# Front end of a decoder layer: which vectors are loaded first, from which queue, and TensorE given work on a zeroed tile

## The chip, the cores and the metric

One Trainium2 chip, one of its cores. The metric is the device time of one execution in microseconds. Five engines of the core run their own instruction streams and meet at semaphores: TensorE (PE), VectorE (DVE), ScalarE (ACT), GpSimd (POOL) and SyncE (SP). SP, ACT and POOL can issue DMA transfers.

## The reference, cut to what matters

One layer of a decoder with 256 tokens and 2048 channels, in float32:

```python
u = rms_norm(x, mix_norm_pre)            # over channels, then a gain per channel
proj = u @ w_in
c_q, c_kv, k_r, z, xbc, dt_raw, g_attn, g_ssm = split_cols(proj, IN_SPLITS)
attn = mla_branch(c_q, c_kv, k_r, cos, sin, q_norm, w_uq, kv_norm, w_ukv)
ssm = mamba2_branch(z, xbc, dt_raw, conv_w, conv_b, dt_bias, a_log, d_skip, ssm_norm)
mixed = sigmoid(g_attn) * (attn @ w_attn_o) + sigmoid(g_ssm) * (ssm @ w_ssm_o)
h = x + rms_norm(mixed @ w_out, mix_norm_post)
# then a SwiGLU block (ffn_norm_pre, ffn_norm_post) and a gated
# embedding block (ple_norm_pre, ple_norm_post), each added to h
```

The first part of the state-space branch puts a causal convolution of width 4 (`conv_w`, `conv_b`) on the columns x, B and C of the projection.

## The kernel before, in words

Activations are held with channels on the 128 partitions and the 256 tokens beside them. `u` has 16 such tiles, each twice: `u[:, kt, 0]` is the rounded high part (float32r), `u[:, kt, 1]` the remainder. Weights come in chunks of [128, 1024] floats through a ring of four slots (`raw`): ScalarE writes the high part `whi`, VectorE the remainder `wlo`, and TensorE does three matmuls for each tile (`mm3`: high by high, high by low, low by high). Chunks are worked off in an order written out by hand in `PHASES`: first "bc" (4 chunks, the B and C columns of one group), then "ssm" (8 rounds of 20 chunks; the first four of round 0 are half as wide and hold the rope and dt columns), then the others. Each engine's stream names the chunks in this order and puts its other work between them. SP loads chunk n when `lo_ready` says that VectorE has split chunk n − 4; TensorE begins a chunk when it has been split. "bc" chunks are loaded without a wait.

The front end works like this. SP loads x, tokens on partitions, as four transfers (`x_tok`, two blocks of 128 tokens, two halves of columns; semaphores `x_in00` to `x_in11`), then the first "bc" chunk, then eight transfers of parameter vectors into `rows`, then the other weights. ACT's queue loads the constants (`cst`: identity, triangle, ones) and four more vectors; POOL's queue loads three vectors of the heads (`dtb`, `alog`, `dsk`). For each block of tokens ScalarE and VectorE sum the squares of one half of the columns each (L944, L1356), the inverse root follows (L935, L937, `newton` at L1345 to L1347), and VectorE puts it on a diagonal, `dg` (L1366). TensorE multiplies x by this diagonal, which transposes and scales at once (`x_transposed`, L475): seven banks of PSUM for block 0, then block 1, the eighth bank at the end. Bank 7 is used in between for four transposes of `rows` (L488), which bring all parameter vectors onto the partitions. VectorE copies them to `pv_all` (L1369) and the 104 columns that are kept to `pv` (L1371). With them ScalarE makes `u` high (L956) and VectorE `u` low (L1376), two tiles a bank, with the splits of the four "bc" chunks (L926, L1325) between them. Then VectorE clears `xdt` (L1384), rearranges the convolution's parameters from `pv_all` into `gp_all` (L1387 to L1397), and only then splits the first "ssm" chunk. TensorE does the "bc" chunks and goes on to `rope_dt_chunk`; the dt columns are transposed in bank 7 (L516). At the start, TensorE's queue raises 13 semaphores (L430).

Of the kernel before, what the change touches and what calls it, by code (L numbers as in the profile page):

```python
# [49 lines left out]
P = 128  # L50
# [30 lines left out]
V_KEEP = 104  # L81
V_CB, V_SN, V_TAP = 104, 152, 184
V_ALL = 376
# [9 lines left out]
def build(nc, x, p_in, positions, mix_norm_pre, mix_norm_post, w_in, q_norm, w_uq, kv_norm, w_ukv,  # L93
# [60 lines left out]
    sq_tok = first("sq_tok", [P, D_MODEL])  # L154
    dg = first("dg", [P, 2, P])
    rows = first("rows", [P, 4, P])
    pv_all = first("pv_all", [P, V_ALL])
# [68 lines left out]
    def bank(b):  # L226
        return psum[:, b, :]
# [118 lines left out]
    def _(sp):  # L346
# [8 lines left out]

        vec = [(ffn_norm_pre, 16, 32), (ffn_norm_post, 16, 48), (ple_norm_pre, 16, 64), (ple_norm_post, 16, 80)]
        for v, n, at_row in vec:
            sp.dma_start(rows[at_row:at_row + n, 0, :], v.rearrange("(t p) -> t p", p=P)) \
                .then_inc(sem("rows_in"), 16)
        sp.dma_start(rows[0:48, 1, :], conv_b.rearrange("(t p) -> t p", p=P)).then_inc(sem("rows_in"), 16)  # L360
        sp.dma_start(rows[48:80, 1, :], ssm_norm.rearrange("(t p) -> t p", p=P)).then_inc(sem("rows_in"), 16)
        for i in range(2):
            sp.dma_start(rows[0:96, 2 + i, :],
                         conv_w[2 * i:2 * i + 2, :].rearrange("a (t p) -> (a t) p", p=P)) \
                .then_inc(sem("rows_in"), 16)
        for phase, (per, its) in PHASES.items():
# [31 lines left out]
    @block.gpsimd  # L398
    def _(pool):
        for v, dst in ((dt_bias, dtb), (a_log, alog), (d_skip, dsk)):  # L400
            pool.dma_start(dst[:, :], v.partition_broadcast(P)).then_inc(sem("heads_in"), 16)
# [26 lines left out]
    def _(pe):  # L428
# [43 lines left out]
        def x_transposed(b, blk):  # L472
# [5 lines left out]
            if blk:  # L478
                last.then_inc(sem("xt_mm"), 1)

        pe.wait_ge(sem("dg_ready"), 1)
        for b in range(7):
            x_transposed(b, 0)
        pe.wait_ge(sem("cst_in"), 16)
        pe.wait_ge(sem("rows_in"), 12 * 16)
        at_col = 0
        for i, n in enumerate((V_KEEP, 80, 96, 96)):
            last = T.transpose(bank(7)[:, at_col:at_col + n], rows[0:n, i, :], cst[0:n, 0:n])  # L488
            at_col += n
        last.then_inc(sem("pv_mm"), 1)  # L490
        pe.wait_ge(sem("dg_ready"), 2)
# [6 lines left out]
        for c_ in range(4):  # L498
            pe.wait_ge(sem("u_lo"), 4 * c_ + 4)
            chunk("bc", 0, c_, (0, 1), u, range(4 * c_, 4 * c_ + 4), c_ == 0, c_ == 3)  # L500

        def rope_dt_chunk(c_):
# [9 lines left out]
        def dt_by_tokens():  # L512

            pe.wait_ge(sem("kr_ev"), 1)
            for blk in range(2):
                last = T.transpose(bank(7)[:, 64 * blk:64 * blk + 64], kr[64:P, blk * P:blk * P + P], cst[64:P, 64:P])  # L516
            last.then_inc(sem("dt_mm"), 1)
# [395 lines left out]
    def _(act):  # L913
        S.preload_act_table_set("natural_log_exp_and_others")
        act.dma_start(cst[:, :], cst_in).then_inc(sem("cst_in"), 16)
        for v, n, at_row in ((mix_norm_pre, 16, 0), (mix_norm_post, 16, 16), (q_norm, 4, 96), (kv_norm, 4, 100)):
            act.dma_start(rows[at_row:at_row + n, 0, :], v.rearrange("(t p) -> t p", p=P)) \
                .then_inc(sem("rows_in"), 16)

# [32 lines left out]
        for b in range(8):  # L952
            act.wait_ge(sem("xt_mm"), b + 1)
            for k in range(2):
                kt = 2 * b + k
                S.activation(u[:, kt, 0, :], bank(b)[:, k * SEQ:k * SEQ + SEQ], ACT.Identity,  # L956
                                 scale=pv_all[:, V_MIXPRE + kt:V_MIXPRE + kt + 1]).then_inc(sem("u_hi"), 1)
            if b in (0, 2, 4, 6):
                split("bc", 0, b // 2)
# [360 lines left out]
    def _(dve):  # L1320
# [31 lines left out]


        for b in range(2):
            dve.wait_ge(sem(f"x_in{b}1"), 16)
# [8 lines left out]
            if b == 0:  # L1364
                dve.wait_ge(sem("cst_in"), 16)
            V.tensor_scalar(dg[:, b, :], ident, st0[:, b, 4:5], None, ALU.mult).then_inc(sem("dg_ready"), 1)  # L1366

        dve.wait_ge(sem("pv_mm"), 1)
        V.tensor_copy(pv_all[:, :], bank(7)[:, 0:V_ALL]).then_inc(sem("pv_ev"), 1)  # L1369
        dve.wait_ge(sem("pv_ev"), 1)  # L1370
        V.tensor_copy(pv[:, :], pv_all[:, 0:V_KEEP]).then_inc(sem("pv_kept"), 1)  # L1371
        for b in range(8):
            dve.wait_ge(sem("u_hi"), 2 * b + 2)
            for k in range(2):
                kt = 2 * b + k
                V.scalar_tensor_tensor(u[:, kt, 1, :], bank(b)[:, k * SEQ:k * SEQ + SEQ],  # L1376
                                           pv_all[:, V_MIXPRE + kt:V_MIXPRE + kt + 1],
                                           u[:, kt, 0, :].bitcast(F32), ALU.mult, ALU.subtract) \
                                               .then_inc(sem("u_lo"), 1)
# [3 lines left out]

        link(V.memset(xdt[:, :, :, 64:128], 0.0))  # L1384
        taps = pv_all[:, V_TAP:V_ALL].rearrange("p (a n) -> p a n", a=4)
        gp_taps = gp_all[:, :, 0:24].rearrange("p g (a t) -> p a g t", t=6)
# [649 lines left out]
```

## Time and profile before

| | |
|---|---|
| median of 3 runs | 2198.53 us (2197.8 to 2199.4) |
| profiled execution | 2199.38 us |
| its span, first to last instruction | 2197.6 us |
| TensorE busy | 2149.7 us, 98% of the span |
| VectorE, ScalarE busy | 1326.4 us (60%), 1075.8 us (49%) |
| mean granted TensorE clock | 0.993 |

In rows of the timeline an instruction stands as start, duration, engine, line of the kernel, operation, output<-input with shapes, and a count if several follow each other; in brackets how long the engine was idle before it and what released it. A float32 matmul leaves two records. TensorE overlaps instructions, so a record's duration is longer than the distance to the next.

### The profile page before, as it was taken

How to read it: one execution, taken by the hardware profiler on the slowest of the kernel's cores; microseconds unless marked ns; L12 is line 12 of the kernel's file. 1: busy time of each engine (PE TensorE's matmuls, PEld its weight loads, DVE VectorE, ACT ScalarE, POOL GpSimd, SP SyncE). 2: the span in 40 equal slices, each digit the busy share in tenths (PEclk: the TensorE clock that was granted, in tenths of full speed). 3: DMA queues.
4: the chain of work that ended last, by engine and by line, in shares of the span. 5: the costliest groups of instructions: out<-in, count | busy, mean ns of one | idle time of the engine just before them, and what ended most of it. 6: DMA issues, size and time to landing. Idle time of an engine off the chain costs nothing.

```text
span 2197.6 us, 41147 instructions
## 1 busy us (share of the span) xinstructions
PE 2149.7 (98%) x15558; PEld 2033.8 (93%) x15558; DVE 1326.4 (60%) x1902; ACT 1075.8 (49%) x1311; POOL 9.6 (0%) x21
## 2 busy tenths in 40 slices
PE   7999999999999999999999989999999999999997
PEld 7999999999999999999999978888888888888896
DVE  5767777767664444676455457566666664444655
ACT  5555556555554444344444455444444444344653
POOL 0000000000000000000000000000000000000000
PEclk9999999999999999999999999999999999999998
DMA  7665665555555555445556535666666655555452
GB/s 208 192 177 161 187 185 163 174 179 162 172 174 182 179 183 177 125 120 161 183 182 213 189 115 170 192 187 189 188 191 186 191 189 183 184 182 193 152 163 86
DMA packets 411419, 382.85 MB, mean 174 GB/s; under 512 B 25864, under 2 KB 407296, under 8 KB 410080
## 3 DMA queue, kind: packets, MB, share of 16 engines
q1 hardware_dynamic: 409360, 370.37, 55.3%
q0 software_dynamic: 1776, 11.44, 1.6%
q8 instruction: 41, 0.67, 0.1%
q10 hardware_dynamic: 224, 0.22, 0.0%
q14 instruction: 18, 0.15, 0.0%
HBM read 379.81 MB, written 2.16 MB: 174 GB/s over the span
## 4 chain that ended last, share of the span: by engine, by line
PE 95%; DVE 2%; ACT 1%; issue 1%; DMA 0%; SPq 0%; ACTq 0%; DVEq 0%
PE acc L454 22%; PE acc L434 18%; PE acc L436 18%; PE acc L435 18%; PE acc L456 11%; PE acc L727 1%; PE acc L799 1%; PE acc L552 1%; PE acc L558 1%; PE acc L563 1%; PE acc L661 0%; PE acc L662 0%; DVE wlo L1325 0%; ACT whi L926 0%; DVE bt L1850 0%
## 5 line engine op out<-in xcount | busy, mean ns | idle before, releaser
L1325 DVE TENSOR_TENSOR wlo<-raw,whi 128x1024 fp32r<-128x1024 f32 (+1 forms) x712 | 853.1, 1202 | 660.8 <-ACT whi L926 658.2
L926 ACT ACTIVATE whi<-raw 128x1024 fp32r<-128x1024 f32 (+1 forms) x712 | 735.6, 1040 | 668.0 <-PE acc L436 386.8
L434 PE MATMUL acc<-u,whi 128*128 128x256 f32 x2192 | 630.6, 288 | 2.9 <-DVE wlo L1325 1.7
L436 PE MATMUL acc<-u,wlo 128*128 128x256 f32 x2192 | 620.3, 283 | 0.0
L435 PE MATMUL acc<-u,whi 128*128 128x256 f32 x2192 | 620.2, 283 | 0.0
L454 PE MATMUL acc<-u,whi 128*128 128x512 f32 x1408 | 490.2, 395 | 0.0
L434 PEld LDWEIGHTS acc<-u,whi 128*128 128x128 f32 x2192 | 420.5, 192 | 5.5 <-DVE wlo L1325 1.6
L435 PEld LDWEIGHTS acc<-u,whi 128*128 128x128 f32 x2192 | 420.4, 192 | 1.2
L436 PEld LDWEIGHTS acc<-u,wlo 128*128 128x128 f32 x2192 | 420.3, 192 | 0.0
L456 PE MATMUL acc<-u,wlo 128*128 128x256 f32 x1408 | 390.5, 277 | 0.0
L454 PEld LDWEIGHTS acc<-u,whi 128*128 128x128 f32 x1408 | 264.6, 188 | 61.4
L434 PE MATMUL acc<-g,whi 128*128 128x256 f32 x1024 | 290.9, 284 | 2.5 <-DVE wlo L1325 2.5
L436 PE MATMUL acc<-g,wlo 128*128 128x256 f32 x1024 | 289.8, 283 | 0.0
L435 PE MATMUL acc<-g,whi 128*128 128x256 f32 x1024 | 289.8, 283 | 0.0
L456 PEld LDWEIGHTS acc<-u,wlo 128*128 128x128 f32 x1408 | 264.8, 188 | 0.2
L454 PE MATMUL acc<-g,whi 128*128 128x512 f32 x704 | 248.4, 398 | 1.5 <-issue 1.5
L434 PEld LDWEIGHTS acc<-g,whi 128*128 128x128 f32 x1024 | 196.5, 192 | 3.4 <-DVE wlo L1325 3.3
L456 PE MATMUL acc<-g,wlo 128*128 128x256 f32 x704 | 197.7, 281 | 0.0
L435 PEld LDWEIGHTS acc<-g,whi 128*128 128x128 f32 x1024 | 196.5, 192 | 0.0
L436 PEld LDWEIGHTS acc<-g,wlo 128*128 128x128 f32 x1024 | 196.5, 192 | 0.0
L454 PEld LDWEIGHTS acc<-g,whi 128*128 128x128 f32 x704 | 132.2, 188 | 34.3 <-issue 1.8
L456 PEld LDWEIGHTS acc<-g,wlo 128*128 128x128 f32 x704 | 133.0, 189 | 0.0
(277 smaller groups left out, 1610.7 us busy)
## 6 DMA issues: line engine op xcount, KB each, us to landing
raw<-w_in_in SPq DMA_DIRECT2D x208, 512.0 KB, 3.8
raw<-w_gate_in SPq DMA_DIRECT2D x88, 512.0 KB, 4.3
raw<-w_up_in SPq DMA_DIRECT2D x88, 512.0 KB, 4.5
raw<-w_ssm_o_in SPq DMA_DIRECT2D x64, 512.0 KB, 3.5
raw<-w_down_in SPq DMA_DIRECT2D x64, 512.0 KB, 3.5
raw<-w_in_in SPq DMA_DIRECT2D x64, 256.0 KB, 4.0
raw<-w_attn_o_in SPq DMA_DIRECT2D x32, 512.0 KB, 3.5
raw<-w_out_in SPq DMA_DIRECT2D x32, 512.0 KB, 4.5
```

Source lines behind the costliest of these rows:

```text
L434: T.matmul(o, wh, xh, start=start, stop=False, skip_group_check=True)
L435: T.matmul(o, wh, xl, start=False, stop=False, skip_group_check=True)
L436: return T.matmul(o, wl, xh, start=False, stop=stop, skip_group_check=True)
L454: T.matmul(bank(b), wh[:, j, i * P:i * P + P], src[:, kt, :, :].rearrange("p a s -> p (a s)"), start=start and j == 0, stop=False, skip_gr ...
L456: last = T.matmul(bank(b)[:, 0:SEQ], wl[:, j, i * P:i * P + P], src[:, kt, 0, :], start=False, stop=stop and j == len(kts) - 1, skip_group ...
L552: T.matmul(bank(b)[:, 0:256], xdt[:, 0, p, 0:128], ea[:, 0:256], start=True, stop=False, skip_group_check=True)
L558: T.matmul(bank(b)[:, 0:256], xdt[:, 0, p, 64:192], eb[:, 0:256], start=False, stop=True, skip_group_check=True).then_inc(sem("y_mm"), 1)
L563: last = T.matmul(bank(7)[:, 0:256], ones, sq[:, t, :], start=t == 0, stop=t == 3)
L727: last = T.matmul(o, c[:, 4 + j, a_, t], w_[:, j, :], start=j == 0 and blk == 0 and n_ == 0, stop=j == 3 and n_ == 2 and blk == 1, skip_gr ...
L799: last = T.matmul(bank(6)[:, 0:SEQ], ones, sq_n[:, j % 2, i, :], start=j == 0 and i == 0, stop=j == 7 and i == 1, skip_group_check=True)
L926: S.activation(whi[:, slot, 0:w], raw[:, slot, 0:w], ACT.Copy).then_inc(sem("hi_ready"), 1)
L1325: V.tensor_tensor(wlo[:, slot, 0:w], raw[:, slot, 0:w], whi[:, slot, 0:w].bitcast(F32), ALU.subtract) \
```

## The change

Of the parameter vectors, only `mix_norm_pre` is loaded at the start (ACT's queue, its own semaphore `pre_in`). The eleven other transfers into `rows` go to POOL's queue, ahead of the three head vectors, and POOL issues them when the last quarter of x is in. TensorE gets 32 matmuls on a tile `warm` that VectorE sets to zero, then transposes `mix_norm_pre` alone, then the x blocks. VectorE copies the 16 columns of `mix_norm_pre` between `dg` 0 and block 1. The four transposes of `rows` come after the "bc" chunks on TensorE, and the copies of `pv_all` and `pv` after the clearing of `xdt` on VectorE. `dt_by_tokens` waits for the copy too, since it writes bank 7. ScalarE and VectorE take the gain of `u` from `pv`.

```diff
@@ -153,6 +153,7 @@
     x_tok = first("x_tok", [P, 2, D_MODEL])
     sq_tok = first("sq_tok", [P, D_MODEL])
     dg = first("dg", [P, 2, P])
+    warm = first("warm", [P, P])
     rows = first("rows", [P, 4, P])
     pv_all = first("pv_all", [P, V_ALL])
     st0 = first("st0", [P, 2, 8])
@@ -353,16 +354,6 @@
             sp.dma_start(raw[:, 0, :].rearrange("p (t n) -> p t n", t=4)[:, :, o:o + STATE], src) \
                 .then_inc(raw_in[0], 16)
 
-        vec = [(ffn_norm_pre, 16, 32), (ffn_norm_post, 16, 48), (ple_norm_pre, 16, 64), (ple_norm_post, 16, 80)]
-        for v, n, at_row in vec:
-            sp.dma_start(rows[at_row:at_row + n, 0, :], v.rearrange("(t p) -> t p", p=P)) \
-                .then_inc(sem("rows_in"), 16)
-        sp.dma_start(rows[0:48, 1, :], conv_b.rearrange("(t p) -> t p", p=P)).then_inc(sem("rows_in"), 16)
-        sp.dma_start(rows[48:80, 1, :], ssm_norm.rearrange("(t p) -> t p", p=P)).then_inc(sem("rows_in"), 16)
-        for i in range(2):
-            sp.dma_start(rows[0:96, 2 + i, :],
-                         conv_w[2 * i:2 * i + 2, :].rearrange("a (t p) -> (a t) p", p=P)) \
-                .then_inc(sem("rows_in"), 16)
         for phase, (per, its) in PHASES.items():
             def load(it, c):
                 slot = c % RING
@@ -397,6 +388,18 @@
 
     @block.gpsimd
     def _(pool):
+        pool.wait_ge(sem("x_in11"), 16)
+        vec = [(mix_norm_post, 16, 16), (ffn_norm_pre, 16, 32), (ffn_norm_post, 16, 48), (ple_norm_pre, 16, 64),
+               (ple_norm_post, 16, 80), (q_norm, 4, 96), (kv_norm, 4, 100)]
+        for v, n, at_row in vec:
+            pool.dma_start(rows[at_row:at_row + n, 0, :], v.rearrange("(t p) -> t p", p=P)) \
+                .then_inc(sem("rows_in"), 16)
+        pool.dma_start(rows[0:48, 1, :], conv_b.rearrange("(t p) -> t p", p=P)).then_inc(sem("rows_in"), 16)
+        pool.dma_start(rows[48:80, 1, :], ssm_norm.rearrange("(t p) -> t p", p=P)).then_inc(sem("rows_in"), 16)
+        for i in range(2):
+            pool.dma_start(rows[0:96, 2 + i, :],
+                           conv_w[2 * i:2 * i + 2, :].rearrange("a (t p) -> (a t) p", p=P)) \
+                .then_inc(sem("rows_in"), 16)
         for v, dst in ((dt_bias, dtb), (a_log, alog), (d_skip, dsk)):
             pool.dma_start(dst[:, :], v.partition_broadcast(P)).then_inc(sem("heads_in"), 16)
 
@@ -478,16 +481,15 @@
             if blk:
                 last.then_inc(sem("xt_mm"), 1)
 
+        pe.wait_ge(sem("warm_set"), 1)
+        for _ in range(32):
+            T.matmul(bank(7)[:, 0:P], warm[:, :], warm[:, :], start=True, stop=True)
+        pe.wait_ge(sem("cst_in"), 16)
+        pe.wait_ge(sem("pre_in"), 16)
+        T.transpose(bank(7)[:, 0:16], rows[0:16, 0, :], cst[0:16, 0:16]).then_inc(sem("pv_mm"), 1)
         pe.wait_ge(sem("dg_ready"), 1)
         for b in range(7):
             x_transposed(b, 0)
-        pe.wait_ge(sem("cst_in"), 16)
-        pe.wait_ge(sem("rows_in"), 12 * 16)
-        at_col = 0
-        for i, n in enumerate((V_KEEP, 80, 96, 96)):
-            last = T.transpose(bank(7)[:, at_col:at_col + n], rows[0:n, i, :], cst[0:n, 0:n])
-            at_col += n
-        last.then_inc(sem("pv_mm"), 1)
         pe.wait_ge(sem("dg_ready"), 2)
         for b in range(7):
             x_transposed(b, 1)
@@ -498,6 +500,13 @@
         for c_ in range(4):
             pe.wait_ge(sem("u_lo"), 4 * c_ + 4)
             chunk("bc", 0, c_, (0, 1), u, range(4 * c_, 4 * c_ + 4), c_ == 0, c_ == 3)
+
+        pe.wait_ge(sem("rows_in"), 11 * 16)
+        at_col = 0
+        for i, n in enumerate((V_KEEP, 80, 96, 96)):
+            last = T.transpose(bank(7)[:, at_col:at_col + n], rows[0:n, i, :], cst[0:n, 0:n])
+            at_col += n
+        last.then_inc(sem("pv_mm"), 1)
 
         def rope_dt_chunk(c_):
 
@@ -512,6 +521,7 @@
         def dt_by_tokens():
 
             pe.wait_ge(sem("kr_ev"), 1)
+            pe.wait_ge(sem("pv_ev"), 2)
             for blk in range(2):
                 last = T.transpose(bank(7)[:, 64 * blk:64 * blk + 64], kr[64:P, blk * P:blk * P + P], cst[64:P, 64:P])
             last.then_inc(sem("dt_mm"), 1)
@@ -913,9 +923,7 @@
     def _(act):
         S.preload_act_table_set("natural_log_exp_and_others")
         act.dma_start(cst[:, :], cst_in).then_inc(sem("cst_in"), 16)
-        for v, n, at_row in ((mix_norm_pre, 16, 0), (mix_norm_post, 16, 16), (q_norm, 4, 96), (kv_norm, 4, 100)):
-            act.dma_start(rows[at_row:at_row + n, 0, :], v.rearrange("(t p) -> t p", p=P)) \
-                .then_inc(sem("rows_in"), 16)
+        act.dma_start(rows[0:16, 0, :], mix_norm_pre.rearrange("(t p) -> t p", p=P)).then_inc(sem("pre_in"), 16)
 
         def split(phase, it, c):
 
@@ -954,7 +962,7 @@
             for k in range(2):
                 kt = 2 * b + k
                 S.activation(u[:, kt, 0, :], bank(b)[:, k * SEQ:k * SEQ + SEQ], ACT.Identity,
-                                 scale=pv_all[:, V_MIXPRE + kt:V_MIXPRE + kt + 1]).then_inc(sem("u_hi"), 1)
+                                 scale=pv[:, V_MIXPRE + kt:V_MIXPRE + kt + 1]).then_inc(sem("u_hi"), 1)
             if b in (0, 2, 4, 6):
                 split("bc", 0, b // 2)
 
@@ -1351,6 +1359,7 @@
                 link(ins)
 
 
+        V.memset(warm[:, :], 0.0).then_inc(sem("warm_set"), 1)
         for b in range(2):
             dve.wait_ge(sem(f"x_in{b}1"), 16)
             link(V.tensor_tensor_reduce(out=sq_tok[:, 1024:2048], in0=x_tok[:, b, 1024:2048],
@@ -1364,17 +1373,17 @@
             if b == 0:
                 dve.wait_ge(sem("cst_in"), 16)
             V.tensor_scalar(dg[:, b, :], ident, st0[:, b, 4:5], None, ALU.mult).then_inc(sem("dg_ready"), 1)
-
-        dve.wait_ge(sem("pv_mm"), 1)
-        V.tensor_copy(pv_all[:, :], bank(7)[:, 0:V_ALL]).then_inc(sem("pv_ev"), 1)
+            if b == 0:
+                dve.wait_ge(sem("pv_mm"), 1)
+                V.tensor_copy(pv[:, 0:16], bank(7)[:, 0:16]).then_inc(sem("pv_ev"), 1)
+
         dve.wait_ge(sem("pv_ev"), 1)
-        V.tensor_copy(pv[:, :], pv_all[:, 0:V_KEEP]).then_inc(sem("pv_kept"), 1)
         for b in range(8):
             dve.wait_ge(sem("u_hi"), 2 * b + 2)
             for k in range(2):
                 kt = 2 * b + k
                 V.scalar_tensor_tensor(u[:, kt, 1, :], bank(b)[:, k * SEQ:k * SEQ + SEQ],
-                                           pv_all[:, V_MIXPRE + kt:V_MIXPRE + kt + 1],
+                                           pv[:, V_MIXPRE + kt:V_MIXPRE + kt + 1],
                                            u[:, kt, 0, :].bitcast(F32), ALU.mult, ALU.subtract) \
                                                .then_inc(sem("u_lo"), 1)
             if b in (0, 2, 4, 6):
@@ -1382,6 +1391,10 @@
 
 
         link(V.memset(xdt[:, :, :, 64:128], 0.0))
+        dve.wait_ge(sem("pv_mm"), 2)
+        V.tensor_copy(pv_all[:, :], bank(7)[:, 0:V_ALL]).then_inc(sem("pv_ev"), 1)
+        dve.wait_ge(sem("pv_ev"), 2)
+        link(V.tensor_copy(pv[:, 16:V_KEEP], pv_all[:, 16:V_KEEP]))
         taps = pv_all[:, V_TAP:V_ALL].rearrange("p (a n) -> p a n", a=4)
         gp_taps = gp_all[:, :, 0:24].rearrange("p g (a t) -> p a g t", t=6)
         V.tensor_copy(gp_taps[:, :, :, 0:4], taps[:, :, 0:32].rearrange("p a (g t) -> p a g t", t=4))
```

## Rows read from the trace of the kernel before

**Rows 1.** The page, part 1: busy time, share of the span and instructions.

```profile
PE 2149.7 (98%) x15558; PEld 2033.8 (93%) x15558; DVE 1326.4 (60%) x1902; ACT 1075.8 (49%) x1311; POOL 9.6 (0%) x21
```

**Rows 2.** TensorE's waits over the whole span, longest first.

```profile
PE acc L475 <- DVE dg L1366: 11.1, 1, 11.1
```

**Rows 3.** The chain of waits, 0 to 60 us: start, us, what.

```profile
1.33 6.80 DMA x_tok<-x_in
...
11.07 6.29 PE acc L475 x28
17.36 0.34 PE acc L488 x4
17.73 0.56 DVE pv_all L1369
18.31 0.84 ACT u L956 x2
...
22.19 0.39 PE acc L434
```

**Rows 4.** Instructions in order of time, 12 to 34 us: start, us, what.

```profile
12.55 1.23 DVE L1356 CUSTOM_DVE_ANT_0 sq_tok<-x_tok 128x1024 f32<-128x1024 f32 x1 [1.54 <-DMA x_tok<-x_in]
...
15.12 0.28 DVE L1366 TENSOR_SCALAR dg<-cst,st 128x128 f32<-128x128 f32 x1
...
17.20 0.49 PE L488 MATMUL acc<-cst,rows 104*128 104x104 f32 x4
...
18.31 0.21 DVE L1371 COPY pv<-pv_all 128x104 f32<-128x104 f32 x1
...
33.81 0.28 PE L434 MATMUL acc<-u,whi 128*128 128x256 f32 x1
```

**Rows 5.** VectorE, then ScalarE, in order of time, 30 to 38 us.

```profile
30.82 0.23 DVE L1387 COPY gp_all<-pv_all 128x128 f32<-128x128 f32 x1
...
31.87 0.69 DVE L1325 TENSOR_TENSOR wlo<-raw,whi 128x512 fp32r<-128x512 f32 x1
...
37.39 1.22 DVE L1325 TENSOR_TENSOR wlo<-raw,whi 128x1024 fp32r<-128x1024 f32 x1 [1.96 <-ACT whi L926]
...
36.30 1.06 ACT L926 ACTIVATE whi<-raw 128x1024 fp32r<-128x1024 f32 x1 [1.59 <-DMA raw<-w_in_in]
```

**Rows 6.** L475 alone in two stretches: length, PE busy, PEld busy, PEclk, DMA, GB/s.

```profile
11.07:17.36 6.29, 6.29 (x28) 6.04 (x28) 1.00 1.14 269
17.53:21.74 4.21, 4.21 (x36) 4.02 (x36) 1.00 0.43 107
```

**Rows 7.** Instructions in order of time, around 1305 and 2175 us.

```profile
1304.63 2.05 PE L799 MATMUL acc<-sq_n,cst 128*128 128x256 f32 x4 [8.64 <-ACT sq_n L1185]
...
1307.00 2.08 PE L799 MATMUL acc<-sq_n,cst 128*128 128x256 f32 x4 [0.32 <-ACT sq_n L1185]
...
2175.22 1.13 PE L837 MATMUL acc<-sq_n,cst 128*128 128x256 f32 x4 [1.97 <-ACT sq_n L1290]
```

**Rows 8.** Stretches: busy time by engine, then PEclk, DMA share and GB/s.

```profile
1299.00:1301.00 2.00, 0.00 (x0) 0.00 (x0) 0.89 (x3) 1.00 (x2) 0.00 (x0) 0.90 0.71 239
1310.00:1311.00 1.00, 1.00 (x5) 0.90 (x4) 1.00 (x3) 0.00 (x0) 0.00 (x0) 0.58 0.06 16
...
2175.00:2180.00 5.00, 1.13 (x4) 0.68 (x4) 1.33 (x4) 3.57 (x5) 0.00 (x0) 0.78 0.00 0
```

**Rows 9.** The source line L430 alone: durations in ns, first and last start.

```profile
L430 PEldq EVENT_SEMAPHORE  x13: 51/51/51, 1.0 to 2.8; - x13
```

**Rows 10.** Instructions in order of time, 117 to 119 us.

```profile
117.58 1.22 DVE L1325 TENSOR_TENSOR wlo<-raw,whi 128x1024 fp32r<-128x1024 f32 x1 [0.65 <-ACT whi L926]
117.61 0.55 POOL L408 DMA_DIRECT2D cumb<-cum_scratch  x1 [39.53 <-DVE e L1465]
```

**Rows 11.** DMA issues, 0 to 120 us: size of one, median us to landing.

```profile
cum_scratch<-cumt POOLq DMA_DIRECT2D x1, 64.0 KB, 3.2
...
dsk<-d_skip_in POOLq DMA_DIRECT2D x1, 32.0 KB, 8.1
```

## The prediction

> **What bounds the kernel now.** I read the page's busy shares first. TensorE is busy for 98% of the span [rows 1], so nearly all of the time is one dense stream of matmuls. A change to the front end can only shift the start of that stream or put holes in it. Next I read TensorE's waits: the longest, 11.1 us, stands before its first instruction [rows 2]. Then the chain of waits over the front [rows 3], to see which work fills the time before the main stream. It runs: x from DRAM to 8.19 us, the sum of squares and its root on VectorE and ScalarE, the first diagonal `dg`, 28 TensorE records on L475 from 11.07 for 6.29 us, the row transposes (L488), the copy of `pv_all` at 17.73, the first two `u` tiles on ScalarE at 18.31, one weight split on each of ScalarE and VectorE, two `u_lo` tiles, and the first main matmul at 22.19. From there matmuls start every 0.12 us to the end of the "bc" work (96 of them), and the rope/dt chunk follows at 33.81 without a gap [rows 4]. The last reading is what VectorE does between, since the change moves work into that place: it finishes `u_lo`, clears `xdt`, fills `gp_all` from 30.82 to 31.87 and has the first rope/dt split ready at about 32.56, 1.25 us before TensorE needs it [rows 5].
>
> **The change part by part.**
>
> *The work on the zeroed tile.* The first 14 diagonal matmuls (28 records) take 11.07 to 17.20, 0.438 us each; the last 18 (36 records) take 4.21 us, 0.234 each [rows 6]. The granted clock in the profile reads 1.00 in both stretches, but the pace of the first is about half that of the second, as between 1.2 and 2.4 GHz. The engine had been idle before the first, and had worked 6.13 us when the pace rose. Later in the trace the clock is seen at 0.50 while matmuls restart at 1304.63; from 1307.00 they run nearly without a stop, and in the stretch 1310 to 1311 the clock reads 0.58, so it rose at about 1310.84, 3.84 us after 1307.00 [rows 7, 8]. I take these two as bounds for the slow stretch of the new work and 5 us, about their middle, as its value.
>
> TensorE can't start at zero: its queue is busy with 13 semaphore instructions whose last starts at 2.8 [rows 9], so the new work begins at 2.85. (The memset of `warm` on an idle VectorE is over well before.) With 5 us slow, 11.4 matmuls are done at 7.85 and the other 20.6 take 4.82 us: end at 12.67. With 3.84 us the end is at 12.1, with 6.13 at 13.2. Then the one transpose of `mix_norm_pre` and its copy on VectorE: no row has either; from the start of the four L488 transposes to the copy of their result 0.53 us pass (17.20 to 17.73), and the smallest copy there takes 0.21 [rows 3, 4]. I take 0.35 and 0.20, 0.55 together, so the vector is ready at 13.2 (12.65 to 13.75).
>
> *VectorE's new wait.* That wait stands between `dg` 0 and the sum of squares of the second half of x. Before, this sum starts at 12.55, when x lands [rows 4]. Behind it are the mean, the root and `dg` 1, ready at 15.40, 2.85 us later. Now it starts at 13.2: 0.67 us later (0.1 to 1.2). If x lands sooner because fewer small transfers lie beside it, it changes nothing, since the copy is later. The transposes of the first half of x, 14 at 0.234, run from 12.7 to 16.0 beside it.
>
> *What is gained.* ScalarE starts `u` at 18.31, held by slow matmuls and by the twelve vector loads, the transposes and the big copy. Now it needs only `dg` 1 and two more matmuls. With `dg` 1 at 15.40 this would be 15.40 + 0.05 + 4 records at 0.112 + about 0.25 to drain = 16.10, a gain of 2.21. Less the 0.67, the gain is **1.54 us** (1.0 to 2.1). From there to the first main matmul the same 3.88 us pass, for ScalarE and VectorE are dense in it. The weights are no obstacle: the first wait on their transfer is seen at 36.30 [rows 5], and SP now issues them earlier, having eight fewer loads in front.
>
> *The vectors on POOL's queue.* They start when x is in, 12.55. An issue costs POOL 0.54 us, so the eleventh is out at 18.5; the landing of a POOL load took 3.2 to 8.1 us [rows 10, 11], so the rows are in by 21.7 to 26.6. TensorE asks for them at 33.81 − 1.54 = 32.27. The cover is 5.7 us or more, and the cost nothing; with the cover gone it would be one for one. The three head loads behind them, issued by 20.1, land by 28.2, and VectorE asks for them after 33. Against this queue one could fear that POOL can't issue while VectorE works. The row says otherwise: the POOL issue at 117.61 took 0.55 us beside a VectorE split that started at 117.58 [rows 10]. By it the cost stays nothing; were POOL held, it would be rival 4, and the sum 5.6 us more. (The Trainium skill, SBUF — State Buffer, section "SBUF: two separate sides", warns of this: GpSimd writes the descriptors of the loads it issues, and is locked out of a port it shares with VectorE during certain operations of it, fp32 copies within SBUF above all. Whether copies do this no row here shows.)
>
> *The hand-off.* This is the term that I think decides. The four big row transposes now stand on TensorE behind the last "bc" chunk. On VectorE the wait for them stands ahead of the fill of `gp_all`, and this ahead of the first rope/dt split. That split is what TensorE needs next. So VectorE first sits idle, and then its chain lies bare: transposes to copy 0.53 [rows 4]; copy of `pv_all` to its use 0.58 (17.73 to 18.31); the copy into `pv` 0.21 and 0.03; the fill of `gp_all` 1.05 (30.82 to 31.87); the split and its signal 0.72. Together **3.11 us**, from 32.27 to 35.38. Before it was 0, TensorE going on at 33.81. The net at this point is −1.54 + 3.11 = **+1.57 us**.
>
> *One echo.* SP loads slot 0 again when the first rope/dt split is done, 32.56 before. Those weights, the fifth chunk, landed at 36.30 and were split at 38.61; TensorE needed them 48 matmuls of 0.12 after 33.81, at 39.57: slack 0.96. The split now ends at 35.36, 2.80 later, and TensorE only 1.57 later: slack 0.96 + 1.57 − 2.80 = −0.27. So a stall of **0.27** (0 if the transfer is quicker). I take it to end there, for the next chunk has 2.88 us more of TensorE's time (24 matmuls) before it is needed. Everything after follows TensorE, for SP, POOL and the splits wait on its or VectorE's progress.
>
> **Sum.** −1.54 + 3.11 + 0.27 = +1.84 us. With the bounds of the gain and of the echo: +1.0 to +2.4. The profiled execution had a span of 2197.6 and a time of 2199.38; the same sum gives a span of 2199.4. Its time lies 0.85 above the median, 2198.53, with the three runs 1.6 apart. The forecast is 2198.5 + 1.8 = **2200.3 us**, +0.08%. A measurement of this kernel can tell about 0.2% from no change, 4.4 us, so I forecast no change.
>
> **The rivals.**
>
> 1. *The hand-off costs nothing.* If the split were ready anyway, only the transposes, 0.37 us on TensorE (17.36 to 17.73), would be added: −1.54 + 0.37 = −1.2, 2197.4. Against it is the order of VectorE's queue; for it, only that TensorE had no stall here before. 0.10.
>
> 2. *The clock falls in the hand-off.* TensorE is idle from about 32.7 to 35.4, 2.7 us. After an idle time of 1.97 us at 2175.22 the clock still read 1.00; in an idle time of 8.64 it fell, about 4.6 us in (0.90 over 1299 to 1301), and in the stretch from 2175 it fell (0.78) about 1.4 us after a short burst that itself followed that 1.97 [rows 7, 8]. 2.7 is nearer to the case where it held. Were it lost for as long as at the front, 6.13 us for 14 matmuls instead of 14 x 0.234 = 3.28 would cost 2.85, and hide the echo: 1.57 + 2.85 = +4.4, 2202.9, on the edge of 0.2%. The point is an idle time long enough for a fall. 0.13.
>
> 3. *The zeroed tile does not raise the pace* (the change does not do what it says). Then 32 x 0.438 = 14.0, to 16.9, and the vector is ready at 17.4; `dg` 1 comes at 20.3, the first half of x takes its slow 6.13 to 23.1, and ScalarE starts at 23.7, 5.4 later than now. With 3.11 for the hand-off and 0.27 that is +8.8, 2207.3: slower. Against it: the diagonal matmuls have a moving tile that is zero in 127 of 128 places, and the pace rose in them [rows 6]. 0.04.
>
> 4. *POOL can't issue while VectorE works.* VectorE is nearly without a pause until `u` is done, some 28.8 in the new time. Eleven issues behind that end at 34.7 and land at 37.9 at the soonest, where TensorE asks at 32.27: 5.6 us more, 2205.9, slower. It decides from the point where the loads are more than 5.7 us late. Against it stands the issue at 117.61 [rows 10]; the rule of the Trainium skill named above speaks for it. 0.03.
>
> **How the numbers follow.** The forecast has 0.70. The range takes the forecast's own bounds, 2199.5 to 2200.9, and reaches down to rival 1 and up to rival 2: 2197.2 to 2203.2, with some 0.08 left out and the rest of the gap for the spread of the runs. Slower by over 0.2%: rivals 3 and 4, 0.07, and half of rival 2, 0.07: 0.14. Faster by over 0.2% would need 4.4 us: the main stream would have to start at 17.8 with no hand-off, when `dg` 1 alone is at 15.4 and 3.88 us must follow it; 0.02. Within: 0.84.
>
> **What would show it.** In the profile after: matmuls on `warm` from 2.9, slow then fast, ending at 12.1 to 13.2; the second sum of squares starting after a wait on TensorE rather than on x; the first main matmul at 20.1 to 21.2; a wait of TensorE on the VectorE split of some 2.5 to 3 us near 35, the longest of the first 100 us; rows landed by 27; a wait of 0.3 near 41. The forecast is wrong if that wait is missing, if the granted clock reads 0.50 behind it, or if the pace on `warm` never rises.

## The result and the profile after

The changed kernel took 2201.0 us (median of 20 runs, 2198.1 to 2202.9), the kernel before 2197.7 (2194.0 to 2199.4), a ratio of 1.0017 with a 95% interval of 1.0010 to 1.0024. It is some 3.7 us slower by the ratio, 3.3 by the medians. That is inside the range and within 0.2%, but about twice the +1.84 of the sum. What came on top, by the profiles below, is the fall of the clock, which the forecast had as a rival.

The page of the changed kernel, its span and its busy times:

```profile
span 2197.9 us, 41282 instructions
...
PE 2155.4 (98%) x15623; PEld 2042.6 (93%) x15623; DVE 1326.5 (60%) x1904; ACT 1075.6 (49%) x1311; POOL 15.1 (1%) x32
```

The span is only 0.3 us longer than before. This can't be read as the cost of the change, because both kernels have a stretch near the end that takes one of two lengths. The load of `p_tok` is issued when TensorE ends the feed-forward gate and up chunks. Here it is in the timeline of the kernel before, then of the changed one:

```profile
1803.61 0.72 POOL L424 DMA_DIRECT2D p_tok<-p_in  x1 [605.70 <-PE acc L456]
```

```profile
1807.39 0.73 POOL L427 DMA_DIRECT2D p_tok<-p_in  x1 [605.40 <-PE acc L459]
```

At this point the changed kernel is 3.78 us late. From there to the end the kernel before needed 2197.6 − 1803.6 = 394.0 us and the changed one 2197.9 − 1807.4 = 390.5. In all twelve profiles of this study the remainder is either 390.4 to 390.5 (eight) or 394.0 (four, the kernel before among them), whatever was changed in front, and the granted clock reads the same. In the changed kernel SP's 96 loads of `w_down` spread over 246.4 us, in the kernel before over 249.5, so it lies in that stage. What decides it is open. A span can be compared only with this taken off; below I compare events in front.

TensorE's waits in the changed kernel, longest first (total, times, longest), here the third and the fourth; the first two come after 1290 us and are in the kernel before too:

```profile
...
PE acc L437 <- DVE wlo L1333: 6.9, 7, 2.7
PE acc L486 <- issue: 2.9, 1, 2.9
```

The wait of 11.1 us [rows 2] is down to 2.9, since TensorE works on zeros. A wait of 2.7 us on a weight split is new: before, the longest of that kind was 1.0. The front in order of time:

```profile
0.98 0.17 DVE L1362 MEMSET warm<- 128x128 f32 x1 [0.98 <-PEq L2017]
...
2.92 9.39 PE L486 MATMUL acc<-warm 128*128 128x128 f32 x64 [2.92 <-issue]
...
7.08 1.23 DVE L1365 CUSTOM_DVE_ANT_0 sq_tok<-x_tok 128x1024 f32<-128x1024 f32 x1 [5.94 <-DMA x_tok<-x_in]
...
10.03 0.64 POOL L395 DMA_DIRECT2D rows<-mix_norm_post_in  x1 [9.45 <-DMA x_tok<-x_in]
...
12.51 0.17 DVE L1378 COPY pv<-acc 128x16 f32<-128x16 f32 x1 [2.57 <-PE acc L489]
...
12.60 1.22 DVE L1365 CUSTOM_DVE_ANT_0 sq_tok<-x_tok 128x1024 f32<-128x1024 f32 x1
...
15.16 0.28 DVE L1375 TENSOR_SCALAR dg<-cst,st 128x128 f32<-128x128 f32 x1
...
16.34 0.84 ACT L964 ACTIVATE u<-acc,pv 128x256 fp32r<-128x256 f32 x2 [1.79 <-PE acc L478]
...
20.22 0.38 PE L437 MATMUL acc<-u,whi 128*128 128x256 f32 x1 [0.41 <-DVE u L1385]
```

x is in much sooner than before: the first sum of squares of VectorE starts at 7.08 instead of 8.16, and POOL, which waits for the last quarter of x, issues at 10.03, while before VectorE had this quarter only at 12.55 [rows 4]. VectorE then sits idle 2.57 us for the copy at 12.51, which waits for the 32 matmuls. Its second sum starts at 12.60, `dg` 1 is done at 15.44, `u` starts at 16.34 instead of 18.31 [rows 3], the first main matmul at 20.22 instead of 22.19: 1.97 us gained.

The hand-off to the rope/dt chunks, VectorE then TensorE:

```profile
32.43 0.55 DVE L1395 COPY pv_all<-acc 128x376 f32<-128x376 f32 x1 [3.62 <-PE acc L507]
...
34.30 0.69 DVE L1333 TENSOR_TENSOR wlo<-raw,whi 128x512 fp32r<-128x512 f32 x1
...
35.05 0.58 PE L437 MATMUL acc<-u,whi 128*128 128x256 f32 x1 [2.73 <-DVE wlo L1333]
```

TensorE was idle 2.73 us and starts at 35.05, where it had started at 33.81 [rows 4]. Then what the sum left out. Stretches of one microsecond: length, busy time of PE, PEld, DVE, ACT and POOL, granted clock, DMA share, GB/s:

```profile
34.00:35.00 1.00, 0.00 (x0) 0.00 (x0) 0.93 (x4) 0.00 (x0) 0.00 (x0) 0.72 0.00 0
35.00:36.00 1.00, 0.95 (x4) 0.95 (x5) 0.96 (x3) 0.00 (x0) 0.00 (x0) 0.50 0.03 8
...
40.00:41.00 1.00, 1.00 (x7) 1.00 (x7) 0.97 (x1) 0.36 (x1) 0.00 (x0) 0.50 0.95 293
41.00:42.00 1.00, 1.00 (x9) 1.00 (x9) 0.27 (x1) 0.69 (x1) 0.00 (x0) 0.87 1.08 373
```

The granted clock falls within 34 to 35, in the idle time, to 0.50 (1.2 GHz), and comes back at about 41.3. Matmuls start every 0.21 us in between, and every 0.12 ahead of it and behind it. This is rival 2. The vectors, for their part, were in time. The landing times of the loads on L395 (us, least, median, most):

```profile
DMA to landing us min/median/max: 4.3/4.7/4.9
```

The last row load is out at 15.65, so all are in by about 20.

### The profile page after: what moved, and what is told of

Same layout as the page of the kernel before. It is cut to its first block, busy times and chain, and to the rows that moved or that the text cites. A ratio compares the mean times of both kernels' runs of the same rounds, so it can differ in the third digit from the quotient of the medians.

```text
span 2197.9 us, 41282 instructions
## 1 busy us (share of the span) xinstructions
PE 2155.4 (98%) x15623; PEld 2042.6 (93%) x15623; DVE 1326.5 (60%) x1904; ACT 1075.6 (49%) x1311; POOL 15.1 (1%) x32
## 3 DMA queue, kind: packets, MB, share of 16 engines
q0 software_dynamic: 2128, 11.62, 1.6%
## 4 chain that ended last, share of the span: by engine, by line
PE 95%; DVE 2%; ACT 1%; issue 1%; ACTq 0%; DVEq 0%
PE acc L457 22%; PE acc L437 18%; PE acc L439 18%; PE acc L438 18%; PE acc L459 11%; PE acc L737 1%; PE acc L809 1%; PE acc L562 1%; PE acc L568 1%; PE acc L573 1%; PE acc L671 0%; PE acc L672 0%; DVE wlo L1333 0%; PE acc L486 0%; DVE bt L1863 0%
```

## The experiments

To separate the parts I use two lengths of each profile: when the first main matmul starts (front), and from there to the transposes of dt (L516 before), which stand behind ten chunks of TensorE's work and so hold the hand-off, its echo and the clock.

| kernel | first main matmul | from there to dt | dt transposes at | median us | ratio to before (95%) |
|---|---|---|---|---|---|
| before | 22.19 | 23.23 | 45.42 | 2197.7 | |
| changed | 20.22 | 29.25 | 49.47 | 2201.0 | 1.0017 (1.0010 to 1.0024) |
| e1 changed, again | 20.85 | 28.03 | 48.88 | 2199.3 | 1.0014 (1.0005 to 1.0024) |
| e2 split first | 20.11 | 23.58 | 43.69 | 2193.6 | 0.9998 (0.9989 to 1.0007) |
| e3 eleven matmuls in the hand-off | 20.86 | 27.25 | 48.11 | 2197.0 | 1.0010 (1.0001 to 1.0019) |
| e9 five matmuls in the hand-off | 19.62 | 26.95 | 46.57 | 2196.9 | 1.0008 (0.9999 to 1.0017) |
| e4 no zeroed tile | 19.16 | 29.24 | 48.40 | 2198.4 | 1.0017 (1.0008 to 1.0026) |
| e5 split first, no zeroed tile | 19.98 | 23.59 | 43.57 | 2196.7 | 0.9996 (0.9987 to 1.0005) |
| e6 split first, 16 matmuls | 17.80 | 23.57 | 41.37 | 2192.1 | 0.9982 (0.9973 to 0.9991) |
| e7 before + 32 matmuls | 21.06 | 23.22 | 44.28 | 2197.6 | 0.9999 (0.9990 to 1.0008) |
| e8 before, head loads late | 20.82 | 23.23 | 44.05 | 2196.2 | 0.9994 (0.9985 to 1.0003) |
| e10 before, head loads late, 16 matmuls | 18.65 | 23.82 | 42.47 | 2192.5 | 0.9983 (0.9974 to 0.9992) |

Each was timed eleven times in five rounds beside the kernel before, whose medians there were 2195.4 to 2195.7. The intervals are wide for the effects, because the two lengths near the end put up to 3.5 us of chance into every run; the two lengths of the profile carry most of the verdicts. (One of the eleven times of e1 was 12033 us and is left out of its ratio.)

### e1: the changed kernel again

No edit.

> The changed kernel again, timed beside the kernel before and the three below. Theory A (the clock falls in the hand-off): +4 us against before, in the profile 2.7 us of waiting before the first rope/dt matmul, then a granted clock of 0.50 for some 6 us and a distance of 0.21 us between matmuls, and the transposes of dt (45.42 before) at about 49.5. Theory B (forecast as written: only the idle time counts, and the slow stretch in the one profile is chance): +1.2 to +2.4 us in most runs, dt transposes at about 46.9.

TensorE at the start of the main stream and behind the hand-off, then stretches (length, TensorE busy, granted clock, DMA, GB/s):

```profile
20.85 0.38 PE L437 MATMUL acc<-u,whi 128*128 128x256 f32 x1 [0.41 <-DVE u L1385]
...
35.68 0.55 PE L437 MATMUL acc<-u,whi 128*128 128x256 f32 x1 [2.72 <-DVE wlo L1333]
```

```profile
35.00:36.00 1.00, 0.32 (x1) 0.87 0.00 0
...
38.00:39.00 1.00, 1.00 (x6) 0.50 1.07 377
39.00:40.00 1.00, 1.00 (x10) 0.92 1.08 372
```

The idle time is the same, 2.72 us, and the clock falls again, this time at about 35.7, just as the matmuls start, and is back at about 39.2: 3.4 us low instead of 6.8. The dt transposes come 3.5 us later than before (4.1 in the first profile). So it falls both times, but what it costs differs from run to run. Theory A; its mark of 49.5 was missed by 0.6, for this shorter stretch.

### e2: VectorE splits three rope/dt chunks first

```diff
@@ VectorE
         link(V.memset(xdt[:, :, :, 64:128], 0.0))
+        for c_ in range(3):
+            split("ssm", 0, c_)
         dve.wait_ge(sem("pv_mm"), 2)
...
         for c_ in range(20):
-            split("ssm", 0, c_)
+            if c_ >= 3:
+                split("ssm", 0, c_)
```

> VectorE makes the first three rope/dt splits before it waits for the row transposes. Theory A and the hand-off: TensorE goes from the bc chunks through the four transposes (0.35 us) to the first rope/dt matmul without waiting, at about 32.2 against 33.81 before and 35.05 in the changed kernel; the clock stays at 1.00; the time is 1.5 us below before and 5.5 below the changed kernel. Rival (the front end of the changed kernel costs time elsewhere, for instance by late vectors or weights): a wait of 1 us or more appears in the first 60 us all the same, and the time stays above before.

TensorE in order of time:

```profile
31.61 0.28 PE L439 MATMUL acc<-u,wlo 128*128 128x256 f32 x1
31.73 0.49 PE L507 MATMUL acc<-cst,rows 104*128 104x104 f32 x4
32.00 0.37 PE L437 MATMUL acc<-u,whi 128*128 128x256 f32 x1
```

There is no wait: the last bc matmul at 31.61, the row transposes, the first rope/dt matmul at 32.00. The second length is 23.58, 0.35 over before, which is the transposes. The median of 2193.6 stands 1.8 us below that of before in the same rounds; the interval of the ratio reaches 1, so the runs alone don't show it. Against the changed kernel in the same rounds it is 5.6 us by the medians and 3.5 by the ratios, and against the changed kernel's first ratio the intervals don't touch. The dt transposes come 5.2 to 5.8 us sooner than in the changed kernel. The hand-off and what follows it are the whole loss.

### e3 and e9: work for TensorE in the hand-off

```diff
@@ TensorE, behind the four row transposes
         last.then_inc(sem("pv_mm"), 1)
+        for _ in range(11):          # e9: range(5)
+            T.matmul(bank(5)[:, 0:P], warm[:, :], warm[:, :], start=True, stop=True)
```

> The changed kernel with 11 matmuls on the zeroed tile behind the row transposes, which is what TensorE has of idle time there (2.7 us); nothing else needs them. Theory A: the first rope/dt matmul still starts at about 35.1, but the clock stays at 1.00, the dt transposes come at about 46.9 and the time falls by 2.7 us against the changed kernel, to +1.3 against before. Theory B (idle time alone, no clock): no change against the changed kernel, or slower by what the eleven run over.

> The changed kernel with five matmuls on the zeroed tile behind the row transposes instead of eleven, so that some 1.5 us of idle time are left ahead of the first rope/dt matmul. The granted clock fell 2.1, 2.1 and 3.3 us into the idle time of 2.7 us in the profiles with the hand-off as it is (in the last just as the matmuls began). Theory: 1.5 us is too short for a fall; clock 1.00, an echo of 0.3 to 0.5 us before the fifth chunk, dt transposes at about 47, and the time of the version with eleven. Rival: the fall hangs on how busy TensorE is, not on one idle time; the clock reads 0.50 after it and the dt transposes come at 48.9 to 49.5.

e3, the first rope/dt matmul, the first of the fifth chunk, and a stretch between:

```profile
35.68 0.39 PE L437 MATMUL acc<-u,whi 128*128 128x256 f32 x1 [0.24 <-DVE wlo L1335]
...
42.17 0.39 PE L437 MATMUL acc<-u,whi 128*128 128x256 f32 x1 [0.47 <-DVE wlo L1335]
```

```profile
36.00:37.00 1.00, 1.00 (x11) 1.00 0.47 31
```

e9, the same:

```profile
34.45 0.39 PE L437 MATMUL acc<-u,whi 128*128 128x256 f32 x1 [1.57 <-DVE wlo L1335]
...
40.63 0.38 PE L437 MATMUL acc<-u,whi 128*128 128x256 f32 x1 [0.17 <-DVE wlo L1335]
```

```profile
34.00:35.00 1.00, 0.55 (x4) 0.55 (x5) 0.97 (x3) 0.00 (x0) 0.00 (x0) 1.00 0.00 0
35.00:36.00 1.00, 1.00 (x11) 1.00 (x10) 1.00 (x3) 0.00 (x0) 0.00 (x0) 1.00 0.56 52
```

In e3 TensorE waits 0.24 us and in e9 1.57, and both times the clock reads 1.00 after it. The second length is 27.25 and 26.95, against 28.03 and 29.25 when the clock falls: the fall is worth 0.8 to 2.3 us net. Both show the echo of the forecast, 0.47 and 0.17 us before the fifth chunk (0.27 in the forecast); with the slow clock it is absent, for TensorE then gives the transfer time to arrive. So a sixth to two fifths of the loss in the second length (4.8 and 6.0 us) is the clock. The rest, 3.7 to 4.0, is the hand-off (3.2), its echo and about 0.3 us more. The timeline shows these too: at each wait the idle time counts from the end of the last record, 0.28 us behind its start, where matmuls otherwise follow at 0.12, and the second matmul behind the wait starts 0.22 us after the first instead of 0.12. That makes 0.26 us a wait, of which the hand-off, measured from start to start, already holds 0.16. My mark of 46.9 for e3 was missed by 1.2: it took the front of the first profile, 0.64 sooner than e3's, and left out the echo. In the runs e3 and e9 are 2.2 and 1.8 us above before by their ratios, the changed kernel 3.7 and 3.1; the intervals overlap, so the price of the clock rests on the profiles. e9 says more: here 1.57 us of idle time did not bring the clock down, 2.7 did three times out of three (e4 is the third). (The 3.3 us in the expectation is e1's; counted from the last record's end it is 2.8, so this fall came just after the matmuls had begun.)

### e4 and e5: without the zeroed tile

```diff
@@ TensorE (and the memset of warm on VectorE); e5 has the edit of e2 besides
-        pe.wait_ge(sem("warm_set"), 1)
-        for _ in range(32):
-            T.matmul(bank(7)[:, 0:P], warm[:, :], warm[:, :], start=True, stop=True)
```

> The changed kernel without the 32 matmuls on the zeroed tile. If that work is what brings the main stream forward (1.97 us in the profile): the first main matmul goes back from 20.2 to about 22. Rival (the gain comes from the loads, and the zeroed tile only holds TensorE and the vector of the first gain): the diagonal matmuls start at about 10 and run slow for 3.8 to 6.1 us, dg 1 is ready at about 13.1, and ScalarE starts u at 15.6 to 16.7 where the changed kernel has 16.34, so the first main matmul comes at 19.5 to 20.6 and the time changes by less than 1 us.

> VectorE splits three rope/dt chunks before it waits for the row transposes, and TensorE has no work on the zeroed tile. If the two effects add as the profiles show (first main matmul at 19.16 without the zeroed tile, no idle time in the hand-off, 0.35 us for the transposes): the dt transposes at 42.7 (45.42 before), 2.7 us below before and 1 us below the version with the 32 matmuls. Rival (a late weight chunk or clock gives the gain back, as VectorE and the transfers now have less time): a wait of TensorE before 60 us, and no more than 1.7 us below before.

TensorE in e4, with one stretch behind the hand-off, then TensorE in e5:

```profile
9.99 8.76 PE L478 MATMUL acc<-dg,x_tok 128*128 128x128 f32 x64 [3.35 <-DVE dg L1371]
19.16 0.39 PE L437 MATMUL acc<-u,whi 128*128 128x256 f32 x1 [0.41 <-DVE u L1381]
...
33.99 0.58 PE L437 MATMUL acc<-u,whi 128*128 128x256 f32 x1 [2.72 <-DVE wlo L1330]
...
34.00:35.00 1.00, 1.00 (x4) 1.00 (x5) 0.97 (x3) 0.00 (x0) 0.00 (x0) 0.50 0.03 8
```

```profile
10.03 9.55 PE L478 MATMUL acc<-dg,x_tok 128*128 128x128 f32 x64 [3.15 <-DVE dg L1371]
19.98 0.39 PE L437 MATMUL acc<-u,whi 128*128 128x256 f32 x1 [0.41 <-DVE u L1381]
```

Both contradict the idea that the 32 matmuls bring the stream forward here: without them it did not go back to about 22. The first main matmul starts at 19.16 and 19.98 without them and at 20.22, 20.85, 20.11, 20.86 and 19.62 in five profiles with them, 19.6 against 20.3 in the mean; the two sets overlap, so that they cost something is likely and not shown. The diagonal matmuls start at 10.0 and are slow at first (5.20 us in e4's chain of waits for the 32 records up to the one that frees `u`, 3.78 in the changed kernel's), which costs 1.4 us; but with the 32 matmuls in front they start only at 12.4, 2.4 us later. By the runs e4 is where the changed kernel is, 1.0017 of before. The two profiles differ by 0.8 us, as the pace rose at different times. e5 joins this to e2: the second length adds as forecast, the front was 0.8 later than in e4, and the sum 43.57 missed my 42.7. By the runs e5 can't be told from before.

### e6: split first, 16 matmuls

```diff
@@ TensorE; with the edit of e2
-        for _ in range(32):
+        for _ in range(16):
```

> The same with 16 matmuls on the zeroed tile in place of 32. They should end at 8.5 to 9.6, ahead of dg 0 at 9.94, so that neither TensorE nor VectorE waits for them, and the diagonal matmuls run at the full pace. dg 1 at 13.0, u from 13.7, first main matmul at 17.6, and 4.2 us below before. Rival (the pace falls again in the idle time before dg 0, or the weights are not in by then): first main matmul at 19 or later, and no gain over the version without the zeroed tile.

```profile
2.92 6.05 PE L486 MATMUL acc<-warm 128*128 128x128 f32 x32 [2.92 <-issue]
...
9.98 7.41 PE L478 MATMUL acc<-dg,x_tok 128*128 128x128 f32 x64 [0.84 <-DVE dg L1375]
17.80 0.38 PE L437 MATMUL acc<-u,whi 128*128 128x256 f32 x1 [0.41 <-DVE u L1385]
```

The sixteen end at 8.97, before `dg` 0, and the 0.84 us of idle time cost no pace: the 64 records of the diagonal matmuls take 7.41 us, not 9.55. First main matmul at 17.80 (17.6 forecast), and the time 0.9982 of before, with an interval that ends at 0.9991. This beats both kernels: some 4 us below before and, by the ratios, 7 to 8 below the changed one. With no other difference, the front is at 19.98 without this work (e5), at 17.80 with 16 matmuls and at 20.11 with 32 (e2): what counts is that it ends before `dg` 0 is ready.

### e7 and e8: one part alone on the kernel before

e7 adds the memset and the 32 matmuls to the kernel before and nothing else. e8:

```diff
@@ POOL, kernel before
+        pool.wait_ge(sem("x_in11"), 16)
         for v, dst in ((dt_bias, dtb), (a_log, alog), (d_skip, dsk)):
             pool.dma_start(dst[:, :], v.partition_broadcast(P)).then_inc(sem("heads_in"), 16)
```

> The kernel before with the 32 matmuls on the zeroed tile, nothing else. x lands at 12.5 there, so they end at 12.3 to 12.9 when dg 0 has been ready since 11; block 0 then takes 3.3 us instead of 6.3, the row transposes come at 16.3, u starts at 17.3 instead of 18.3, and the first main matmul at 21.2 instead of 22.19: 1 us below before, no hand-off and clock 1.00. Rival (it is the 32 matmuls that give the changed kernel its 1.3 to 2 us in front): first main matmul at 20.9 or earlier.

> The kernel before, with the three head loads on POOL's queue held until x is in, nothing else. Theory: it is these loads (partition broadcasts, 96 packets that took 11.6% of 16 engines over 15 us) that lie beside x: the second quarter of x at 7.1 instead of 8.2, the last at about 10 instead of 12.5. Rival (it is the eleven vector loads of SP and ACT, or SP's earlier weight loads): x lands at 12 or later as before. Either way the time hardly moves, since the row transposes still follow all of block 0: at most 1.1 us less.

TensorE in e7, then in e8:

```profile
2.92 9.90 PE L484 MATMUL acc<-warm 128*128 128x128 f32 x64 [2.92 <-issue]
...
21.06 0.39 PE L435 MATMUL acc<-u,whi 128*128 128x256 f32 x1 [0.46 <-DVE u L1381]
```

```profile
10.05 5.94 PE L476 MATMUL acc<-dg,x_tok 128*128 128x128 f32 x28 [10.05 <-DVE dg L1367]
...
20.82 0.39 PE L435 MATMUL acc<-u,whi 128*128 128x256 f32 x1 [0.46 <-DVE u L1377]
```

e7 gives 1.13 us in front, as expected, with x at 12.22. e8 gives 1.37 (at most 1.1 forecast) with no work added, just by when three small loads start: the diagonal matmuls begin at 10.05. The runs show neither (both intervals hold 1); the profiles do. POOL, which waits for all of x, goes on at 10.06 in e8 and at 10.03 in the changed kernel, so the eleven other loads did not matter for x. The transfer rate shows the same. Two stretches of the kernel before, then of e8 (last column GB/s):

```profile
7.00:8.00 1.00, 0.00 (x0) 0.00 (x0) 0.00 (x0) 0.49 (x2) 0.00 (x0) 1.00 1.54 223
8.00:9.00 1.00, 0.00 (x0) 0.00 (x0) 0.84 (x1) 0.00 (x0) 0.00 (x0) 1.00 0.48 127
```

```profile
7.00:8.00 1.00, 0.00 (x0) 0.00 (x0) 0.86 (x1) 0.00 (x0) 0.00 (x0) 1.00 1.02 416
8.00:9.00 1.00, 0.00 (x0) 0.00 (x0) 0.59 (x3) 0.31 (x3) 0.00 (x0) 1.00 1.01 384
```

In the kernel before, x comes at 223 and 127 GB/s in these two microseconds, and in e8 at 416 and 384. The three head loads (96 KB in 96 packets) took 11.6% of sixteen engines over the first 15 us, or 0.29 us a packet, while SP's packets took 0.06. The Trainium skill, DMA: Bandwidth & Descriptors, section "SWDGE vs HWDGE vs iDMA", says that the loads of GpSimd and those of SP feed different queues of each transfer engine, which serves them in turn; that fits x being held up by them, but no run here shows how the engines share their time.

### e10: the kernel before with both small edits

```diff
@@ POOL as in e8; TensorE as in e7 with
+        for _ in range(16):
```

> The kernel before with only two edits: the three head loads held until x is in, and 16 matmuls on the zeroed tile in front. All vectors stay where they were, the four row transposes stay between the two blocks of x. Theory (only x's landing and TensorE's pace matter in front, the move of the vectors is not needed): diagonal matmuls from 10.0 at the full pace, row transposes at 13.3, pv_all copied by 14.3, u from 14.4, first main matmul at 18.2, dt transposes at 41.4, as in the version with the split first and 16 matmuls, and 4 us below before. Rival: the vectors on SP's queue are not in by 13.3 (the latest is issued at 9.0), and the front loses what they are late.

```profile
2.92 5.65 PE L485 MATMUL acc<-warm 128*128 128x128 f32 x32 [2.92 <-issue]
10.06 3.39 PE L477 MATMUL acc<-dg,x_tok 128*128 128x128 f32 x28 [1.49 <-DVE dg L1372]
13.62 0.52 PE L493 MATMUL acc<-cst,rows 104*128 104x104 f32 x4 [0.17 <-DMA rows<-conv_w_in]
...
18.65 0.38 PE L436 MATMUL acc<-u,whi 128*128 128x256 f32 x1 [0.46 <-DVE u L1382]
```

The vectors on SP's queue are nearly in time: TensorE waits 0.17 us for the last, the row transposes stand at 13.62, the first main matmul at 18.65 (18.2 forecast). The dt transposes missed my 41.4 by 1.1 us, 0.34 of it a wait before the fifth chunk at 36.52. The ratio is 0.9983 (0.9974 to 0.9992), as good as e6, though e6 is 1.1 us ahead at the dt transposes. So the move of the eleven vectors, and with it the hand-off, was not needed for the gain.

## Why the prediction was right, and where its sum was not

*The work on the zeroed tile.* It ended at 12.2 to 13.0 in five profiles with 32 of them, inside the 12.1 to 13.2 of the bounds, and at 11.7 in a sixth, and the vector was ready at 12.7 (13.2 forecast) in the profile after.

*VectorE's new wait* was found as forecast, ahead of the second sum of squares. The step behind it failed in part: "if x lands sooner ... it changes nothing, since the copy is later" is true of this kernel, but x landed 2.5 us sooner, and so VectorE stood idle 2.57 us behind the 32 matmuls. The forecast took the gain to need the pace that they raise (in rival 3, where it stays low, `u` starts 5.4 us late); e4 shows a front 3.03 us sooner without them. That x would be sooner, and that three loads on POOL's queue had held it (e8), the forecast did not have.

*What is gained*: forecast 1.54 (1.0 to 2.1), measured 1.97 and 1.34 in the two profiles, and 1.33 to 2.57 in all five with the same front. (Its sum, 15.40 + 0.05 + 0.45 + 0.25, is 16.15 and not 16.10, so it should have read 1.49.) That it fits is in part luck: x was 2.5 us sooner than the forecast had it, and the wait for the 32 matmuls took most of that back.

*The vectors on POOL's queue* cost nothing, as forecast: issues of 0.49 to 0.64 us, landings of 3.5 to 4.9. VectorE was at work for 2.4 of the 5.6 us of these issues, and they were no slower then (0.51 and 0.50 us beside its sum of squares, 0.49 while it was idle). Rival 4, and the rule of the Trainium skill behind it, found no support here; no large fp32 copy within SBUF ran beside them, so this is no test of the rule.

*The hand-off*: forecast 3.11 from where TensorE would have gone on. Measured 35.05 − (20.22 + 11.62) = 3.21. It was the right term, and its reading from VectorE's queue was right line by line. Rival 1 is out.

*The echo*: forecast 0.27, measured 0.47 and 0.17 where the clock held, none where it fell.

*The clock.* This is the step that failed, and by the forecast's own last sentence, which calls it wrong if the granted clock reads 0.50 behind the wait. The forecast wrote "2.7 is nearer to the case where it held" and gave the fall 0.13. It fell in every profile with 2.7 us of idle time, with 0.50 for 6.8, 3.4 and 6.8 us, and stayed at 1.57. The row of 1.97 held only that 1.97 is short enough; it said nothing of 2.7, and the row with 8.64 showed a fall after 4.6 without showing that 2.1 would not do. Its third row, a fall 1.4 us into an idle time behind a short burst, spoke for the fall. The price in rival 2, 2.85 in place of an echo of 0.27, is 2.58 net, above the 0.8 to 2.3 that was measured: at the dt transposes the two profiles are 4.05 and 3.46 us late, against +1.84 of the sum and +4.4 of rival 2. The runs' +3.7 lies there too. Where the clock held, e3 and e9 are 2.69 and 1.15 late there, 1.9 in the mean, so the sum's other terms add up. The range held because it reached to this rival, for the forecast's own bounds ended at 2200.9 and the time was 2201.0; and the kernel before was 0.8 us below the 2198.5 that the forecast started from, which is luck.

Between the dt transposes and the load of `p_tok`, every other profile is 0.1 to 1.0 us shorter than the kernel before (e6: 4.05 ahead at the first, 5.07 at the second). Their cause stays open, as does that of the two lengths of the stage after it.

## What to carry to other kernels

When vector preparation is moved behind a stage, look at what the engine that does it must do next: if its next piece is what TensorE waits for, the preparation's whole chain lies bare, and putting a few of those pieces ahead cost nothing here. Price such a hole with the clock in it. That a hole of some length kept the clock elsewhere in the trace is weak evidence: in the kernel before, the clock held in an idle time of 1.97 us and fell 1.4 us after the burst of 1.13 us that followed it [rows 7, 8]. Before adding work that keeps TensorE busy ahead of its input, find what that input waits for, and end the work before the input arrives.

## What the hardware did that I had not expected

Three broadcast loads of 32 KB each on POOL's queue delayed 2 MB of x on SP's queue by 2.5 us (e8); their packets took 0.29 us against 0.06. The granted clock fell 2.1 us into an idle time of 2.7 in two profiles and 0.07 us behind its end in a third, and then read 0.50 for 6.8, 6.8 and 3.4 us, though TensorE was at work for nearly all of it. At the start of the kernel the granted clock reads 1.00 while matmuls run at half pace, so there the pace has to be read, not that column. And in the twelve profiles the down-projection stage takes one of two lengths, 3.5 us apart, without regard to what was changed in front.
